# Constants split ahead of x, the mean behind the first adaLN round, nine adaLN rounds inside the attention, and a closing stage without GpSimd

## The reference

```
def run(x, c, ...):
    for layer in range(2):
        mod = (silu(c) @ ada_w[layer] + ada_b[layer])        # adaLN: 6 x 1024 per sequence
        sh1, sc1, g1, sh2, sc2, g2 = split(mod, 6)
        hmix = rms_norm(x, norm_mix_g) * (1 + sc1) + sh1
        out = attention(hmix) if layer == 0 else gla(hmix)
        x = x + g1 * out
        hffn = rms_norm(x, norm_ffn_g) * (1 + sc2) + sh2
        x = x + g2 * moe(hffn)                               # 64 experts, top 8, and a shared one
    return rms_norm(x, final_g)
```

## Time and profile before

| | |
|---|---|
| median of 3 runs | 1486.76 us (1483.82 to 1491.12) |
| the profiled execution | 1487.98 us, span 1486.2 us |
| PE busy | 1440.1 us, 97% of the span |
| DVE / ACT / POOL busy | 443.0 / 323.0 / 49.3 us |
| granted TensorE clock, mean | 0.993 of full speed |
| HBM traffic | 343 GB/s mean; 509.61 MB moved |

### The profile page before, as it was taken

One profiled execution on the slowest core, in us unless ns is written; L12 is line 12 of the kernel. 1 busy time (PEld: TensorE's weight loads), 2 busy tenths in 40 slices (PEclk: granted clock), 3 DMA queues, 4 the chain that ended last, 5 costly groups with the idle time before them and its releaser, 6 DMA issues.

```text
span 1486.2 us, 21147 instructions
## 1 busy us (share of the span) xinstructions
PE 1440.1 (97%) x8450; PEld 732.3 (49%) x8450; DVE 443.0 (30%) x1163; ACT 323.0 (22%) x756; POOL 49.3 (3%) x86
## 2 busy tenths in 40 slices
PE   7998999999999999999999999999999999999996
PEld 3345656444444445444465456564444444454443
DVE  1136425221221312121245243442121213222113
ACT  2124314111111111111255222411111111111113
POOL 0100302000000000000000010010000000000000
PEclk9999899999999999999999999999999999999998
DMA  9899406999999999999944252199999999999991
GB/s 395 327 383 388 178 1 265 426 372 429 424 422 426 426 424 425 425 427 423 408 177 187 114 211 87 64 388 393 410 423 425 423 426 425 425 426 425 425 417 50
DMA packets 47893, 509.61 MB, mean 343 GB/s; under 512 B 5777, under 2 KB 6049, under 8 KB 8209
## 3 DMA queue, kind: packets, MB, share of 16 engines
q1 hardware_dynamic: 26784, 364.33, 58.6%
q10 hardware_dynamic: 17280, 125.84, 20.5%
q0 software_dynamic: 3728, 18.07, 3.3%
HBM read 499.16 MB, written 11.01 MB: 343 GB/s over the span
## 4 chain that ended last, share of the span: by engine, by line
PE 90%; DVE 3%; ACT 3%; DMA 2%; issue 1%; ACTq 0%; SPq 0%; DVEq 0%
PE bank L1996 27%; PE banks L2045 13%; PE banks L1898 10%; PE banks L430 5%; PE ybank L1926 4%; PE banks L1926 3%; PE bank L1928 3%; PE banks L1108 3%; PE bank L492 2%; DMA s_gu_ring<-in_moe_up_dram 1%; PE ybank L1690 1%; PE banks L1690 1%; PE banks L685 1%; PE banks L1113 1%; PE banks L659 1%
## 5 line engine op out<-in xcount | busy, mean ns | idle before, releaser
L1996 PE MATMUL bank<-s_gu_ring,s_hbuf 128*32 128x512 f32 (+1 forms) x2752 | 409.4, 593 | 1.2 <-DVE s_hbuf L2126 0.9
L1996 PEld LDWEIGHTS bank<-s_gu_ring,s_hbuf 128*32 128x32 f32 (+1 forms) x2752 | 127.4, 119 | 274.0 <-issue 274.0
L2045 PE MATMUL banks<-s_dn_ring,s_hTs 128*32 128x512 f32 (+1 forms) x1376 | 211.5, 596 | 3.8 <-issue 3.8
L2171 DVE TENSOR_TENSOR s_ylo<-banks,s_yhi 128x512 fp32r<-128x512 f32 x116 | 80.2, 692 | 334.5 <-ACT s_yhi L2087 334.5
L1898 PE MATMUL banks<-s_sel,s_htok 128*128 128x512 f32 (+2 forms) x640 | 149.3, 381 | 0.6 <-issue 0.6
L1898 PEld LDWEIGHTS banks<-s_sel,s_htok 128*128 128x128 f32 x640 | 109.8, 188 | 60.8 <-issue 44.5
L2087 ACT CAST s_yhi<-banks 128x512 fp32r<-128x512 f32 x116 | 67.9, 586 | 308.5 <-PE banks L2045 308.5
L2045 PEld LDWEIGHTS banks<-s_dn_ring,s_hTs 128*32 128x32 f32 (+1 forms) x1376 | 58.8, 119 | 125.4 <-issue 125.4
L2166 DVE SCALAR_TENSOR_TENSOR s_hh<-s_sg,s_wsl,bank 128x256 f32<-128x256 f32 x58 | 27.9, 481 | 298.9 <-ACT s_sg L2078 298.9
L2078 ACT ACTIVATE s_sg<-bank 128x256 f32<-128x256 f32 x58 | 22.3, 384 | 377.3 <-PE bank L1996 377.3
L2126 DVE COPY s_hbuf<-banks 128x512 f32<-128x512 f32 (+1 forms) x60 | 40.4, 674 | 100.4 <-PE banks L1898 100.4
(11 more groups left out here) (460 smaller groups left out, 1483.0 us busy)
## 6 DMA issues: line engine op xcount, KB each, us to landing
s_gu_ring<-in_moe_up_dram SPq DMA_DIRECT2D x128, 2048.0 KB, 17.6
s_dn_ring<-in_moe_wd_dram ACTq DMA_DIRECT2D x120, 1024.0 KB, 18.2
s_gu_ring<-in_ada_w_dram SPq DMA_DIRECT2D x24, 2048.0 KB, 12.1
s_gu_ring<-in_win_dram SPq DMA_DIRECT2D x6, 2048.0 KB, 16.1
s_dn_ring<-in_moe_wd_dram SPq DMA_DIRECT2D x8, 1024.0 KB, 18.8
s_gu_ring<-in_wqkv_dram SPq DMA_DIRECT2D x6, 1024.0 KB, 18.9
s_gu_ring<-in_wo_dram SPq DMA_DIRECT2D x2, 2048.0 KB, 16.8
s_gu_ring<-in_shared_up_dram SPq DMA_DIRECT2D x2, 2048.0 KB, 12.5
```

The source lines that it names most:

```text
L1996: last = pe.matmul(W0[o:o + n, :], tokens_of(p, k)[:, o:o + n], w[:, k, :, :], start=(k == 0), stop=(k == KC - 1))
L2045: last = pe.matmul((W1, W2)[half][o:o + n, :], hTs[:, f, o:o + n], dn_ring[:, dn_of[(l, r)][0], w0:w0 + 512], start=(f == 0), stop=(f == 1))
L2171: dve.tensor_tensor(ylo[:, half, :], (W1, W2)[half], yhi[:, half, :].bitcast(F32), ALU.subtract).then_inc(S["y_low"], 1)
```

## The change

1. The constant table is split. Ahead of x SP loads only `lead` (417 of 1196 columns: 208.5 KB in place of 598 KB). The other 779 columns (`moe`) are loaded by POOL's queue ahead of the router weights.
2. POOL loads the cached keys and values once round 5's tile has landed (before: round 6's).
3. PE runs round 0 ahead of the mean, with three dummies behind the mean in place of five behind the round.
4. Only rounds 4 to 8 stand in the projections. Rounds 9 to 17 stand in steps 0, 1, 2, 4, 6, 8, 10, 15 and 22 of the attention. The groups (7, 8, 9), (10, 11) become (7, 8), (9, 10, 11). Slots and counts of the loads follow: rounds 11 to 17 go to slots 2, 3, 4, 1, 0, 2, 3.
5. The dummies of steps 2 and 4 are gone.
6. Behind the experts of each layer stand two dummies in place of four, and the second half of the sample sums is copied by DVE rather than ACT.
7. In the closing stage DVE multiplies tile 1 and half of tile 2 by `final_g` while ACT still squares; ACT scales them afterwards; DVE does tile 0 and the other half of tile 2 in one instruction each. POOL does nothing, and SP stores all three.

```
-                AT_SLOT = {}
-                AT_SLOT[0] = 11
-                for n, i in zip(range(12, 18), (2, 5, 8, 12, 16, 20)):
-                    AT_SLOT[i] = n
+                AT_SLOT = {i: 9 + x for x, i in enumerate((0, 1, 2, 4, 6, 8, 10, 15, 22))}
...
-                    slot_in[ada_slots[6]].wait(pool, ada_in[6])
+                    slot_in[ada_slots[5]].wait(pool, ada_in[5])
...
-                    mean(pe, 0, bank[4])
                     pe.wait_ge(F["cond"], 2)
                     ada_part(pe, 0)
-                    keep_awake(pe, bank[5], 5)
+                    mean(pe, 0, bank[4])
+                    keep_awake(pe, bank[5], 3)
                     ada_part(pe, 2)
...
-                        if g > 1:
+                        if 1 < g < 7:
                             ada_fold(pe, 2 + g)
-                        if g:
+                        if 0 < g < 6:
                             ada_part(pe, 3 + g)
...
-                        if u == 2:
-                            keep_awake(pe, b, 5)
...
-                        if i in (2, 3):
+                        if i == 3:
                             keep_awake(pe, bank[6], 5)
...
-                    keep_awake(pe, W0, 4)
+                    keep_awake(pe, W0, 2)
...
-                for t in (2, 1):
-                    tn = TILES[t][1]
-                    act.activation(yt[0:tn, t, :], flat_out(t), ACT.Copy, scale=stt[0:tn, 2, t:t + 1]).then_inc(E["scaled"], 1)
+                act.activation(yt[:, 1, :], yt[:, 1, :], ACT.Copy, scale=stt[:, 2, 1:2]).then_inc(E["scaled"], 1)
+                act.activation(yt[0:NS, 2, 0:512], yt[0:NS, 2, 0:512], ACT.Copy, scale=stt[0:NS, 2, 2:3]).then_inc(E["scaled"], 1)
...
-                stream(slot, lambda dst: [...a["wqkv"][cch][:, 0:GUW // 2])], 9 + 2 * cch)
+                stream(slot, lambda dst: [...a["wqkv"][cch][:, 0:GUW // 2])], (9, 11, 12)[cch])
...
-            for n, used in zip(range(4, 12), (5, 6, 7, 8, 10, 12, 14, 15)):
+            for n, used in zip(range(4, 11), (5, 6, 7, 8, 10, 13, 14)):
                 ada_next(n, n % 2, used)
-            for n in range(12, 18):
-                ada_next(n, (n - 10) % NGU, n + 4)
-            units[0] = 3
+            for n, slot in zip(range(11, 18), (2, 3, 4, 1, 0, 2, 3)):
+                ada_next(n, slot, n + 4)
+            units[0] = 4
```

More of the change, by code:

```diff
@@ L95 @@
 CONSTS = dict(
-    all=dict(ident=128, ones=128, slot=128, tie=64, token=448, part=9, ecol=1, keycol=1, keyrow=64, caprow=64, avg=128, fold=32, eps=1),
+    lead=dict(ident=128, ones=128, avg=128, fold=32, eps=1),
+    moe=dict(slot=128, tie=64, token=448, part=9, ecol=1, keycol=1, keyrow=64, caprow=64),
     start=dict(upper=128, upper2=128),
@@ L256, in decoder_step @@
         lay, const_range, _ = const_layout()
-        csts = {"all": sb("cst", [P, const_range["all"][1]])}
+        cst = sb("cst", [P, const_range["moe"][1]])
+        csts = {name: cst[:, const_range[name][0]:const_range[name][1]] for name in ("lead", "moe")}
         vt = sb("vt", [P, 96 + V2_N])
@@ L877, in _ @@
                     token_out(6)
-                    ada_copy(act, 9)
                     for f in range(3, 6):
@@ L2323, in final @@
         def final(c, l, i, acct, gate):
-            E = {n: sem("final_" + n) for n in ("x_psum", "scaled", "sample_full", "y_full", "out")}
+            E = {n: sem("final_" + n) for n in ("x_psum", "scaled", "y_full", "out")}
             g_slot, g_in = stream_next(lambda dst: [(dst[:, 0:2, :].rearrange("p k n -> p (k n)"),
@@ L2356, in _ @@
                     act.wait_ge(E["x_psum"], 4 * (half + 1))
-                    for t, (t0, tn) in enumerate(TILES):
-                        n = 3 * half + t
+                    for x, t in enumerate(((0, 1, 2), (1, 0, 2))[half]):
+                        tn = TILES[t][1]
+                        n = 3 * half + x
                         if n >= 2:
@@ L2373, in _ @@
                 gated_back(dve, l, gate, add)
+                slot_in[g_slot].wait(dve, g_in)
+                dve.wait_ge(N["sq_full"], KC * i + 3)
+                dve.tensor_tensor(yt[0:NS, 2, 0:512], out[2][0:NS, 0, :], g_row[0:NS, 0:512], ALU.mult)
+                dve.wait_ge(N["sq_full"], KC * i + 4)
+                dve.tensor_tensor(yt[:, 1, :], flat_out(1), g_row, ALU.mult)
                 dve.wait_ge(N["sq_full"], KC * i + 6)
@@ L2378, in _ @@
                 dve.wait_ge(N["rstd_full"], i + 1)
-                slot_in[g_slot].wait(dve, g_in)
                 dve.scalar_tensor_tensor(yt[:, 0, :], flat_out(0), stt[:, 2, 0:1], g_row, ALU.mult, ALU.mult).then_inc(E["y_full"], 1)
[L2381 to L2390, removed]
+                dve.scalar_tensor_tensor(yt[0:NS, 2, 512:1024], out[2][0:NS, 1, :], stt[0:NS, 2, 2:3], g_row[0:NS, 512:1024],
+                                         ALU.mult, ALU.mult).then_inc(E["y_full"], 1)
             @block.sync
             def _(sp):
[L2394 to L2398, removed]
+                sp.wait_ge(E["scaled"], 1)
+                sp.dma_start(a["y_prompt"][0, P:2 * P, :], yt[:, 1, :]).then_inc(E["out"], 16)
+                sp.wait_ge(E["y_full"], 2)
+                sp.dma_start(a["y_prompt"][0, 0:P, :], yt[:, 0, :]).then_inc(E["out"], 16)
+                sp.wait_ge(E["scaled"], 2)
+                sp.wait_ge(E["y_full"], 3)
+                sp.dma_start(a["y_sample"].rearrange("b t d -> (b t) d"), yt[0:NS, 2, :]).then_inc(E["out"], 16)
+                sp.wait_ge(E["out"], 48)
             @block.gpsimd
@@ L2502, in front_streams @@
             for cch, slot in enumerate((2, 3, 4)):
-                stream(slot, lambda dst: [(dst[:, 0:4, :].rearrange("p k n -> p (k n)"), a["wqkv"][cch][:, 0:GUW // 2])], 9 + 2 * cch)
+                stream(slot, lambda dst: [(dst[:, 0:4, :].rearrange("p k n -> p (k n)"), a["wqkv"][cch][:, 0:GUW // 2])], (9, 11, 12)[cch])
                 qkv_slots.append(slot)
```

15 lines of the change are left out of this document (8 added, 7 removed).

## The result

| | before | after |
|---|---|---|
| median of five runs | 1486.76 us (1483.33 to 1491.12) | 1470.93 us (1470.5 to 1471.09) |
| ratio of the runs, after to before | | 0.9908, 95% interval 0.9888 to 0.9928 |
| the profiled execution, its span | 1487.98, 1486.2 us | 1470.58, 1468.7 us |
| granted TensorE clock, mean | 0.993 | 0.998 |
| PE busy | 1440.1 us | 1427.9 us |

Its five runs lie within 0.6 us; those of before spread over 7.8. The two medians divide to 0.9893; the ratio of the runs in the table is a little nearer to one. The median of before is itself a draw: over the 71 runs of it taken with the experiments it is 1484.6, and against that the gain is 13.7.

A forecast was written before the change was run, and what follows sets the result against it. PE was taken to hold 90% of the chain, with DMA waits at the start and round 11. Gains 7.0 + 0 + 0.5 + 0.5 + 2.4 = 10.4 us took 1486.76 to 1476.4; range 1469.5 to 1483.

The forecast's parts named there:

- rival A: Attention's end: the clock does not fall at 171.7, since round 17 stands in step 22; 4.1 us more, 1472.3; chance 0.30.
- The start: From x's landing to round 2: fewer constants ahead of x, round 0 before the mean, fewer dummies; 2.1 us gained.
- Cover of 0.6 only: At the start: round 2's tile lands near 17.2 and is used near 17.8, leaving 0.6 us.
- Projections to scores 0: Up to unit 0's scores: rounds 9 and 10 leave this stretch, 3.70 us; scores move from 101.13 to 95.3.
- Steps 0 to 7: Attention from unit 0's to unit 8's scores: 24.0 us in place of 25.17, with two more rounds inside.
- C: Steps 0 to 6: tiles late again, PE's earlier start turns into waiting; 1483.4 us; chance 0.08.
- B: Steps 0 to 7: idle replaces the dummies, as the softmax chain sets the step; 1479.4 us; chance 0.17.
- Steps 8 to 26: Later attention steps: PE's work is the same, no gain or loss; 0, bounds plus and minus 1 us.
- The clock: Attention's end: the fall to 0.50 from 171.7 to 181.3 stays in the forecast; 4.1 us to be had without it.
- D: Steps 11 to 14 and 16 to 21: PE's clock falls without rounds; up to 21 us added, 1497; chance 0.05.
- Behind the experts: After each layer's experts: two dummies fewer, 0.5 us gained per layer, at most 0.7.
- The closing stage: Kernel's end: DVE multiplies early and the last store lands at 1482.8 against 1485.3; 2.4 us gained.

The follow-up runs named there:

- second test: Changed kernel without the dummies of step 3 and those ahead of the transposes in step 7 as well; median 1468.51 us, ratio 0.9887.
- closing alone: Kernel before with only the new closing stage, two dummies behind the experts and the sums' copy on DVE; median 1480.31 us, ratio 0.9969.
- start alone: Kernel before with only the constants split, round 0 ahead of the mean and three dummies; median 1480.03 us, ratio 0.9971.
- rounds alone: Kernel before with only the rounds' new places, groups, slots and key loads, all dummies kept; median 1478.29 us, ratio 0.9961.
- the kernel with the dummies back: Changed kernel with the dummies of steps 2 and 4 put back; median 1473.07 us, ratio 0.9919.

## Why the prediction was right, point by point

**In short.** The terms of the sum came out nearly as forecast: 10.4 us were forecast, and 10.8 is the gain over those runs of before whose mean clock is 0.997 or more. The measured 1470.93 lies 5.5 below the forecast, because a term that the forecast had set to nothing, the falls of the clock, was worth several us. It lies within the range because rival A, held less likely than the forecast (0.30 against 0.40), was in it. That is luck in part: A's reason, the place of round 17, decides how often that fall comes and not whether. Part of the distance, 2.1 us, is the draw of before's median: 1486.76 against 1484.6 over 71 runs.

**The start**: forecast 2.1, measured 2.6. x landed 0.70 earlier (7.58), not 0.93; PE was ready for round 2 at 16.3 in place of 20.15, and waited 1.2 for its tile. "Cover of 0.6 only" for round 2's tile was short: 17.8 was forecast for PE, the tile landed at 17.42, and so the bound changed hands, and what the order of mean and round 0 spares is cover for that tile. Up to 0.7 was held back for a round 0 longer than 2.71; it took 2.2, from 12.65 to 14.82.

**Projections to scores 0**: 3.70 was right for the rounds. Missing was what they hid: ACT's copy of the last projection, 0.88. Scores 0 came at 95.63 (forecast 95.3), the two errors cancelling in part.

**Steps 0 to 7**: forecast 24.0, measured 23.49. PE's work, summed to 21.6, is 21.71; the idle was put at 2.4 and is 1.78. The tiles were early (no wait for a DMA), so C is out; idle took the place of the dummies in small part only (0.86 of 2.62, and 0.29 of 2.62 in the second test), so B is out as well.

**Steps 8 to 26**: "no gain and no loss" holds within its bounds of plus and minus 1. An execution with the old places and no fall takes 50.3 from scores 8 to the output projection, the changed kernel 49.5.

**The clock**: this is the term that the forecast left out. What rival A says happened: no fall at the attention's end, 4.15 us where 4.1 stood. 10.4 and 4.1 make 14.5; the fall near 905, which the profile of before has and that of the changed kernel has not, adds 1.65. The other 1.3 of the 17.5 between the two spans are 0.2 more up to unit 8's scores, 0.8 in steps 8 to 26, and small ones. D did not happen: 49.5 us with rounds only in steps 8, 10, 15 and 22 ran at 1.00.

The Trainium skill (TensorE: Matmul & The Clock Gate, Part 4: PE-mode transpose) says that transposes do not count as a busy PE in the same way as matmuls do. The forecast called these steps made of transposes, and that was wrong: in the 49.5 us the transposes (L769) are 52 of 451 matmuls and 9.5 of 45.5 us busy. So the 1.00 shows that such a share brings no fall, and says nothing of transposes alone.

What the forecast had wrong in kind is that it took one fall, at one place, as fixed. In the code of the kernel before it is drawn anew in each execution: at the attention's end and near 905 in both profiles of before, behind round 11's late tile and at 125 in that of before with round 17 moved (the same code up to there), near 901 but not at the attention's end in that of the closing alone. The changed kernel has none of them in its profile, and its runs spread over 0.6 us. The late tile therefore can cost more than its 1.9 us of waiting.

Two things rest on more than profiles. The spread goes with the rounds: the kernels with the rounds at their new places and round 17 in step 22 spread over 0.5 to 3.0 us, those without over 6.7 to 12.6 (start, closing, round 17 moved alone, before). And round 17 back in step 20 brings the spread back (6.2 us) on the changed kernel. That the late tile's removal takes its own fall away rests on profiles: rounds alone shows none there, start alone and the old kernel with round 17 moved show one. How often each falls was not counted.

Of the fall near 905 the cause is open. It stands each time behind the same wait of 0.62 us of PE for DVE, ahead of the second layer's output projection, and that wait is in the profiles without a fall too. The place in time does not decide: the dummies behind the wait start at 890.71, 893.41, 901.47, 905.01 and 905.31 where it falls, and at 890.07, 893.09 and 904.91, among others, where it does not.

**Behind the experts**: 0.5 for each layer forecast; together with the closing stage 0.5 + 2.4 = 2.9 was forecast for the end, and 2.7 came. The layer boundary gave less: from the first layer's last dummies to the second layer's first sums are 6.18 in place of 6.50, 0.3.

**The closing stage**: DVE's product out of PSUM took 1.23 (1.28 taken; 2.53 before, beside POOL), ACT's scaling 1.15 (1.05 taken), and the last store landed in 4.0 where 3.4 was taken. Source and neighbour of the product changed at once, so which of the two made it 1.3 faster wasn't told apart.

**The sum**: the parts alone multiply to 0.9971 x 0.9961 x 0.9969 = 0.9901; the three together, the kernel with the dummies back, have 0.9919. The difference, 2.7 us, lies within the intervals, so the runs neither show nor exclude that the parts overlap, for instance in the falls that they spare. Where no fall interferes the profiles add up: start alone has the first scores 2.7 earlier, rounds alone 2.8, both together 5.6 (95.50).

## What to carry to other kernels

Read where the granted clock falls in more than one execution before you price it: a stall of a late tile may cost its own length and a fall behind it. A kernel whose times spread by several us, with the mean clock of each run going along, is telling you so. Price each set of dummies by itself: in steps that real work now fills, most of its length is on the path (1.76 and 2.33 of 2.62 us), while those ahead of the output projection, where PE would otherwise stand idle, paid 0.7 us in the one profile without them. When you move work away, list what it hid.

## What the runs showed of the hardware

- A fall at the attention's end, with 9.6 us of it at 0.50 in the earlier trace rows, cost 4.15 us, and the same program has it or not from one execution to the next.
- 0.92 us of idle on PE ahead of the output projection, with small matmuls before it, was followed by 0.50; the changed kernel's 0.88 ahead of the first scores, with dense projections before it, was not. Waits of 0.62 us ahead of the second layer's output projection were followed by 0.50 in five profiles and not in the nine others.
- The mean's two matmuls took 0.81 at 13.4 us in one execution and 1.43 at 14.7 in another, round 0 1.85 against 2.71. That this is the clock is read from these times only: the view's granted clock is 1.00 in both there.
- A store of 256 KB that was issued last, behind two of 512 KB in the same queue, landed in 4.0 us; those two landed in 3.5.
